# Windowed attention with stacked keys, the band added together with the row maximum, and the division on GpSimd, in a hybrid diffusion transformer step

## The reference, cut to what matters

```python
band = jnp.abs(qi + BLOCK - kj) <= WINDOW
s_loc = jnp.einsum('bqhgd,bmhd->bhgqm', q_blk, k_loc).astype(jnp.float32) * SCALE
s_loc = jnp.where(valid, s_loc, NEG_INF)
s_ctx = jnp.einsum('bqhgd,bchd->bhgqc', q_blk, k_ctx).astype(jnp.float32) * SCALE
p = _sink_softmax(jnp.concatenate([s_loc, s_ctx], axis=-1), sink).astype(v.dtype)
return (jnp.einsum('bhgqm,bmhd->bqhgd', p[..., :3 * BLOCK], v_loc)
        + jnp.einsum('bhgqc,bchd->bqhgd', p[..., 3 * BLOCK:], v_ctx))
```

## Time and profile before

| | us |
|---|---|
| median of 3 runs | 692.92 |
| lowest and highest | 692.34, 694.98 |
| the profiled execution | 693.16 |
| its span in the profile | 691.4 |

### The profile page before, as it was taken

How to read it: one execution, slowest core, us unless ns; L and a number is a source line. 1 busy time by engine, 2 the same in 40 slices (tenths; PEclk the granted TensorE clock), 3 DMA queues, 4 the chain that set the end, 5 groups by cost and what they waited for, 6 DMA issues and landing times.

```text
span 691.4 us, 9619 instructions
## 1 busy us (share of the span) xinstructions
PE 556.6 (81%) x3081; PEld 310.5 (45%) x3082; DVE 204.1 (30%) x540; ACT 155.7 (23%) x375; POOL 123.2 (18%) x183
## 2 busy tenths in 40 slices
PE   0569999999889998999973489899999787878700
PEld 0335654444355664455542245454655444444300
DVE  1240321011567774124447311111111011111027
ACT  2520111011145453233331021111111110111132
POOL 1000000003400000100000423333333232331212
PEclk9999999999989999999995599999999999999955
DMA  8999007081599400400054559999999999999073
GB/s 260 404 389 398 25 5 300 1 306 58 137 357 299 62 0 1 153 0 31 30 220 161 209 216 377 410 365 412 409 416 406 396 408 406 410 416 373 29 306 163
DMA packets 56728, 168.11 MB, mean 243 GB/s; under 512 B 11773, under 2 KB 12389, under 8 KB 55793
## 3 DMA queue, kind: packets, MB, share of 16 engines
q1 hardware_dynamic: 48928, 150.71, 57.4%
q0 software_dynamic: 6752, 14.13, 5.7%
q10 hardware_dynamic: 1008, 2.75, 1.0%
HBM read 161.13 MB, written 14.57 MB: 254 GB/s over the span
## 4 chain that ended last, share of the span: by engine, by line
PE 50%; DMA 27%; DVE 9%; SPq 5%; ACT 3%; issue 3%; PEld 1%; PEldq 0%; POOL 0%; ACTq 0%; POOLq 0%; DVEq 0%
DMA ring<-in_w_down_dram 13%; PE ps L595 10%; PE ps L709 10%; PE ps L817 6%; PE ps L496 5%; PE ps L576 5%; DMA w<-in_w_down_dram 4%; DMA ring<-in_w_up_dram 4%; DMA ring<-in_w_in_dram 3%; PE ps L825 3%; PE ps L660 3%; PE ps L577 2%; PE ps L688 2%; SPq L395 2%; PE ps L515 2%
## 5 line engine op out<-in xcount | busy, mean ns | idle before, releaser
L817 PE MATMUL ps<-ring,xt 128*64 128x256 f32 x768 | 95.0, 404 | 18.6 <-DMA ring<-in_w_up_dram 11.9
L817 PEld LDWEIGHTS ps<-ring,xt 128*64 128x64 f32 x768 | 63.2, 145 | 56.8 <-issue 35.6
L595 PE MATMUL ps<-ring,h_t 128*128 128x512 f32 x160 | 69.5, 593 | 0.0
L1259 DVE TENSOR_TENSOR hid<-act_g,ps 128x128 f32<-128x128 f32 x32 | 9.2, 288 | 188.4 <-ACT act_g L1473 188.4
L709 PE MATMUL ps<-ring,mix_t 128*128 128x512 f32 x120 | 53.2, 594 | 0.0
L595 PEld LDWEIGHTS ps<-ring,h_t 128*128 128x128 f32 x160 | 30.1, 190 | 37.6 <-issue 37.6
L817 PE MATMUL ps<-w,xt 128*64 128x256 f32 x352 | 40.4, 382 | 5.9 <-DMA w<-in_w_up_dram 3.6
L825 PE MATMUL ps<-ring,hid_t 128*64 128x512 f32 x176 | 42.6, 605 | 3.0 <-ACT hid_t L1483 2.5
L576 PE MATMUL ps<-ring,h_t 128*128 128x512 f32 x80 | 41.0, 594 | 3.7 <-DVE h_t L970 2.7
L1567 POOL DMA_INDIRECT xg<-h_rows,idx_in x32 | 33.4, 1044 | 28.2 <-POOL idx_in L1564 26.9
L1577 POOL DMA_INDIRECT expert_results<-y_sb,idx_out x32 | 32.8, 1024 | 28.2 <-POOL idx_out L1574 28.2
(11 more groups left out here) (231 smaller groups left out, 690.3 us busy)
## 6 DMA issues: line engine op xcount, KB each, us to landing
ring<-in_w_mod_dram SPq DMA_DIRECT2D x8, 3072.0 KB, 19.6
ring<-in_w_gate_dram SPq DMA_DIRECT2D x22, 1024.0 KB
ring<-in_w_up_dram SPq DMA_DIRECT2D x22, 1024.0 KB
ring<-in_w_down_dram SPq DMA_DIRECT2D x22, 1024.0 KB
w<-in_w_gate_dram SPq DMA_DIRECT2D x10, 1024.0 KB
w<-in_w_up_dram SPq DMA_DIRECT2D x10, 1024.0 KB
w<-in_w_down_dram SPq DMA_DIRECT2D x5, 1024.0 KB
w_6d<-in_w_down_dram SPq DMA_DIRECT2D x5, 1024.0 KB
```

What stands on the lines that cost most here:

```text
L595: last = pe.matmul(ps[:, 4 + u % 4, :], h_t[:, k, i * P:(i + 1) * P], w[:, k, :], start=(k == 0), stop=(k == KC - 1))
L817: last = pe.matmul(bank[fh * SLOT:(fh + 1) * SLOT, 0:FE].rearrange("p (a f) -> p a f", a=2), x_t[:, k % 4, (k // 4) * SLOT:(k // 4 + 1) * ...
```

## The change

The zero-padded key copies become one tensor `k_t` with both key heads stacked on the partitions. `scores` multiplies 64 partitions of queries by 64 partitions of keys for each key head, the two heads in turn, and no mask product follows. A new fp32 tensor `band` (five blocks: zero, `mask_prev`, zero, `mask_next`, zero) is added by VectorE in the same instruction that takes the maximum: `tensor_tensor_reduce`, once for each key head, writes the masked scores from PSUM to `probs` and the maximum to `att_stats`. It lowers to two instructions, the main one and one that writes the maximum. The exponentials then work in place on `probs`, and `scores(t)` waits for `masked`, not for the exponentials. In tile 1 the key blocks are taken in the order 1, 2, 0, so that a stretch of `band` fits. `normalise` ends with the reciprocal; GpSimd multiplies the two halves of `probs`. `turn_p`, `p_out` and `values` stand one step later. In `scatter` the copy of the row numbers stands ahead of the wait for the expert's result.

```diff
-                return [0] + [1 + m for m in range(max(n - 1, 0), min(n + 2, 4))]
+                return ([5], [1, 2, 0], [0, 1, 2, 3], [0, 2, 3, 4], [0, 3, 4])[i]
...
-                        last = pe.matmul(bank[:, pos * P:(pos + cnt) * P], q, k_t[:, a, first * P:(first + cnt) * P],
-                                         start=(z == 0), stop=(z == len(parts) - 1 and not masks),
-                                         skip_group_check=True)
-                    for z, (pos, m) in enumerate(masks):
-                        last = pe.matmul(bank[:, pos * P:(pos + 1) * P], ident_b[:, :], mask_b[:, m, :],
-                                         start=False, stop=(z == len(masks) - 1), skip_group_check=True)
+                runs = ([(0, 5, 1)], [(0, 1, 2), (2, 0, 1)], [(0, 0, 1), (1, 1, 3)], [(0, 0, 1), (1, 2, 3)],
+                        [(0, 0, 1), (1, 3, 2)])[i]
+                for z, (pos, first, cnt) in enumerate(runs):
+                    for a in range(KVH):
+                        half = slice(a * HD, (a + 1) * HD)
+                        last = pe.matmul(ps[:, 2 * (t % 2) + a, pos * P:(pos + cnt) * P],
+                                         q_t[half, g, i * P:(i + 1) * P], k_t[half, first * P:(first + cnt) * P],
+                                         start=(z == 0), stop=(z == len(runs) - 1), skip_group_check=True)
...
-                        pe.wait_ge(exp_done, t - 1)
+                        pe.wait_ge(masked, t - 1)
...
-                if 2 <= t < NT + 2:
-                    turn_p(t - 2)
...
-                if t >= 4 and t % 2 == 0:
-                    values((t - 4) // 2)
+                if 3 <= t < NT + 3:
+                    turn_p(t - 3)
...
+                if t >= 5 and t % 2 == 1:
+                    values((t - 5) // 2)
...
-            for a in range(KVH):
-                last = dve.tensor_copy(k_t[a * HD:(a + 1) * HD, a, 0:P], ps[a * HD:(a + 1) * HD, 3, 128:256])
-            last.then_inc(s_cols, 1)
+            dve.tensor_copy(k_t[:, 0:P], ps[:, 3, 128:256]).then_inc(s_cols, 1)
...
-                link(dve.tensor_reduce(att_stats[:, MX, t, :], ps[:, 2 * (t % 2):2 * (t % 2) + 2, 0:width(t)], AX_X, ALU.max))
+                if t >= 4:
+                    dve.wait_ge(pt_tr, 2 * (t - 4) + 2)
+                for a in range(KVH):
+                    last = dve.tensor_tensor_reduce(probs[:, t % 4, a, 0:width(t)], ps[:, 2 * (t % 2) + a, 0:width(t)],
+                                                    band[:, m_at:m_at + width(t)], 1.0, -3e38, ALU.add, ALU.max,
+                                                    att_stats[:, MX, t, a:a + 1])
+                last.then_inc(masked, 1)
...
-                link(dve.reciprocal(att_stats[:, INV, t, :], att_stats[:, DEN, t, :]))
-                for a in range(KVH):
-                    p = probs[:, t % 4, a, 0:width(t)]
-                    last = dve.tensor_scalar(p, p, att_stats[:, INV, t, a:a + 1], None, ALU.mult)
-                last.then_inc(p_norm, 1)
+                dve.reciprocal(att_stats[:, INV, t, :], att_stats[:, DEN, t, :]).then_inc(inv_made, 1)
...
+                pool.wait_ge(inv_made, t + 1)
+                for a in range(KVH):
+                    p = probs[:, t % 4, a, 0:w]
+                    last = pool.tensor_scalar(p, p, att_stats[:, INV, t, a:a + 1], 1.0, ALU.mult, ALU.mult)
+                last.then_inc(p_norm, 1)
...
-                pool.wait_ge(y_cp, e + 1)
                 pool.tensor_copy(idx_out[:, c, 0:1], dst_row[:, bass.ds(e, 1)]).then_inc(out_idx, 1)
                 pool.wait_ge(out_idx, e + 1)
+                pool.sem_inc(idx_seen, 1)
+                pool.wait_ge(y_cp, e + 1)
                 pool.sem_inc(idx_seen, 1)
```

More of the change, by code:

```diff
@@ L206, in hybrid_dit_step @@
         d0 = region(9 * KB)
-        k_t = sb("k_t", [P, KVH, 6 * P], F32, d0)
+        k_t = sb("k_t", [P, 6 * P], F32, d0)
+        band = sb("band", [P, 5 * P], F32, d0 + 3 * KB)
         v_all = sb("v_all", [P, 6, KVW], F32, d0 + 6 * KB)
@@ L719, in _ @@
             pe.wait_ge(s_cv, 16)
-            for t in range(NT + 3):
+            for t in range(NT + 4):
                 if t < NT:
                     if t >= 2:
-                        pe.wait_ge(exp_done, t - 1)
+                        pe.wait_ge(masked, t - 1)
                     scores(t)
-                if t == NT + 1:
+                if t == NT + 2:
                     out_proj(0, 0)
-                if 2 <= t < NT + 2:
-                    turn_p(t - 2)
-                if t == NT + 2:
+                if 3 <= t < NT + 3:
+                    turn_p(t - 3)
+                if t == NT + 3:
                     out_proj(0, 1)
-                if t >= 4 and t % 2 == 0:
-                    values((t - 4) // 2)
+                if t >= 5 and t % 2 == 1:
+                    values((t - 5) // 2)
             def turn_use(u):
@@ L1010, in keys_out @@
                 c_at = (5 if i == 0 else i) * P
-                for a in range(KVH):
-                    last = dve.tensor_copy(k_t[a * HD:(a + 1) * HD, a, c_at:c_at + P], ps[a * HD:(a + 1) * HD, 3, 0:P])
-                last.then_inc(qk_dve, 1)
+                dve.tensor_copy(k_t[:, c_at:c_at + P], ps[:, 3, 0:P]).then_inc(qk_dve, 1)
             for i in range(TILES):
@@ L1069, in row_max @@
             def row_max(t):
-                g = t % PAIRS
+                i, g = t // PAIRS, t % PAIRS
+                m_at = 2 * P if i == 1 else 0
                 dve.wait_ge(score_mm, t + 1)
-                link(dve.tensor_reduce(att_stats[:, MX, t, :], ps[:, 2 * (t % 2):2 * (t % 2) + 2, 0:width(t)], AX_X, ALU.max))
+                if t >= 4:
[5 more added lines that the diff above has]
+                last.then_inc(masked, 1)
+                dve.wait_ge(masked, t + 1)
                 ns = nsink[:, :].rearrange("p (a g) -> p g a", a=KVH)[:, g]
@@ L1102, in _ @@
                     normalise(t - 1)
-                if t >= 2:
-                    p_out(t - 2)
-            p_out(NT - 1)
+                if t >= 3:
+                    p_out(t - 3)
+            for t in range(NT - 2, NT):
+                p_out(t)
             def gated(i):
@@ L1385, in exps @@
                 act.activation(att_stats[:, ES, t, :], att_stats[:, SA, t, :], ACT.Exp)
-                if t >= 4:
-                    act.wait_ge(pt_tr, 2 * (t - 4) + 2)
                 for a in range(KVH):
-                    last = act.activation(probs[:, t % 4, a, 0:width(t)], ps[:, 2 * (t % 2) + a, 0:width(t)], ACT.Exp,
+                    last = act.activation(probs[:, t % 4, a, 0:width(t)], probs[:, t % 4, a, 0:width(t)], ACT.Exp,
                                           bias=att_stats[:, NM, t, a:a + 1], scale=SCALE,
@@ L1398, in p_out @@
                 w = width(t)
+                act.wait_ge(pt_tr, 2 * t + 1)
                 act.copy(p_t[:, (t // 2) % 2, 0, 0:w // P, t % 2, :],
@@ L1405, in values_out @@
                 act.copy(mix_t[:, g:g + 2, i * P:(i + 1) * P], ps[:, 4, 0:2 * P].rearrange("p (g q) -> p g q", q=P)).then_inc(pv_cp, 1)
-            for t in range(NT + 3):
+            for t in range(NT + 4):
                 if t < NT:
                     exps(t)
-                if 2 <= t < NT + 2:
-                    p_out(t - 2)
-                if t >= 4 and t % 2 == 0:
-                    values_out((t - 4) // 2)
+                if 3 <= t < NT + 3:
+                    p_out(t - 3)
+                if t >= 5 and t % 2 == 1:
+                    values_out((t - 5) // 2)
             def norms(i):
@@ L1548, in _ @@
                     pool.tensor_tensor(gm_v[:, i - 1], gm_v[:, i - 1], gmn_bc[:], ALU.mult).then_inc(gv_ready, 1)
+            INV = 6
+            for t in range(TILES * PAIRS):
+                i = t // PAIRS
+                w = P * (1 if i == 0 else 3 if i in (1, 4) else 4)
+                pool.wait_ge(inv_made, t + 1)
[3 more added lines that the diff above has]
+                last.then_inc(p_norm, 1)
             pool.wait_ge(pt_tr, 2 * TILES * PAIRS)
```

33 lines of the change are left out of this document (7 added, 26 removed).

## The result

The changed kernel takes 685.68 us (median of 4 runs, 684.39 to 686.62) beside 693.95 for the kernel before on the same chip (4 runs, 692.34 to 696.63). The ratio is 0.9873, 95% interval 0.9850 to 0.9896: faster, by 8.8 us (8.3 by the medians) where 4.9 were forecast. The profiled execution took 684.39, its span 682.5 (before 693.16 and 691.4).

What follows compares the result with a forecast made beforehand. TensorE was taken as nearly full and also waiting on an attention loop through three engines. Attention -4.7 and scatter -0.25 from the profiled 693.16 gave 688.2 us, range 685.0 to 694.0.

Steps and rivals of the forecast that it cites:

- hiding behind the weights: Rival: the experts' weight stream ends at its old time, only the scatter's gain is left; 692.9 us, chance 0.08.
- Scores: Attention's score products: 2.22 to 1.35 us for four blocks, gain 0.87; three blocks to 1.12, gain 0.56.
- No overlap: Rival: TensorE works the two row halves off one by one, 2.00 instead of 1.35; +5.4, 693.6 us, chance 0.12.
- Maximum: VectorE in attention: two instructions with short reads, 1.52 instead of 1.24 us, +0.28, bounds +0.13 and +0.51.
- half-rate rival: New VectorE maximum instruction runs at half rate, 2.5 to 2.6 us with reads; +9.3, 697.5 us, chance 0.10.
- Exponentials: ScalarE in attention: reading SBUF instead of PSUM, 633 against 597 ns, twice, +0.07 us.
- Multiplication on GpSimd: Attention's multiplication by the reciprocal: 0.8 us each, 1.6 a step, bounds 1.1 and 2.6, hidden by the later place.
- wait for GpSimd: Rival: GpSimd's multiplications stretch VectorE's offset operations and sums through the shared port; +2.8, 691.0 us, chance 0.08.
- Depth: Transposes, copies and values one step later in attention: counted as zero, within 0.5 us either way.
- The clock: Fall of TensorE's clock in attention: held unlikely; later warming in tiles 0 and 1 could cost 1 us.
- the slow stretch: First tile and start of tile 1, at granted clock 0.67: -0.9 from scores, -0.9 from VectorE's multiplications.
- Scatter: Row-number copy ahead of the wait, counted at the last expert only: -0.25 us, bounds 0 and -1.1.

Runs made afterwards that it cites:

- depth two: Changed kernel with transposes, copies and values two steps behind the scores instead of three: 689.68 us, ratio 0.9955.
- stacked keys alone: Kernel before with stacked keys only, masks still added by products, transposes two steps behind: 690.24 us, ratio 0.9946.
- the copy first: ScalarE's even copy issued ahead of the exponentials: on the kernel before 691.13 us; on the changed kernel with transposes two steps behind 689.51 us.

## Why the prediction was right, and where it was off

**What bounds the kernel** was read rightly: nearly full **and** waiting on a loop. Both halves were measured later, 8.09 of TensorE's own work in a round of 8.50, and 6.06 in one of 7.53 after the change. That the gain is carried on to the end one to one held: from the first output projection to the last result's copy it takes 386.2 us before (270.12 to 656.29) and 385.1 after (262.51 to 647.65), so hiding behind the weights is refuted.

**Scores**: mechanism right, size off. Forecast 1.35 for four blocks and 1.12 for three; measured 1.09 and 0.88. The halves overlap nearly in full, 1.09 for products that took 2.00 unshared. The narrow piece, which I had priced like four transposes (0.65), is what I overpriced: the wide records start 0.33 after the narrow ones. No overlap is refuted (2.0 expected by it).

**Maximum**: +0.08 measured, +0.28 forecast. The instruction and its read were right (0.686 and 0.083 against 0.684 and 0.08), but two in a row overlap, as the two exponentials with their reads do in the earlier trace rows, which I had noted for ScalarE and not applied here. The half-rate rival is refuted.

**Exponentials**: +0.07, as forecast.

The four-block round therefore lost 0.97 instead of 0.52, the three-block round 0.54 (7.38 in the chain before, 255.90 to 263.28) instead of 0.21. If tile 1's rounds moved like tile 4's, that is 4 x 0.45 + 4 x 0.33 = 3.1 us more than forecast.

**Multiplication on GpSimd**: 0.69 instead of 0.8, two in 1.36, hidden as argued. The forecast said what hides it, "Without the later place the transposes ... would be late": with depth two it is in the chain with 1.37. The offset operations were not stretched, so VectorE doesn't wait for GpSimd here.

**Depth** is the step that failed: "I count zero, within 0.5 us either way." The reasoning was that the round has the same members and that the extra iteration at the end has nothing but transposes. The first holds for the length of the round (8.51 with depth three before the change, 7.57 and 7.53 after it), though with GpSimd's multiplication and two steps its members are others. The second does not: with short scores the end of the attention, from step 16 on, takes 15.8 with three steps and 16.9 to 18.0 with two, about 1.2 of it by the loop and in two kernels about as much by the clock. With what lies before step 8, where depth and clock are not told apart, 3 to 6 us hang on the depth.

**The clock** I held unlikely to fall, since it had stayed at 1.00 with 3.04 of 5 us busy. In the changed kernel it stayed from 210 us on (0.99 and 1.00). In the kernels with depth two it did not always: with stacked keys alone TensorE was busy for 3.04 of the 5 us up to 265 at 0.96 and then had 0.70, with the copy first 2.76 at 1.00 and then 0.66, while the changed kernel with depth two, with 2.75, kept 1.00. The row that I had leaned on doesn't rule a fall out.

**Where the rest of the gain lies.** Counted from the first maximum, the attention is 9.8 us shorter, where the forecast had 4.7: to step 8 4.2 (19.45 to 15.27; forecast about 2.2, the two 0.9 and tile 1's 0.4), from there to step 16 4.2 (32.89 to 28.69; forecast 2.1), and behind it 1.4 (17.15 to 15.76; forecast 0.4). So the middle came out double by the scores and the maximum, and the ends by more than that. In this pair of profiles the later start takes 2.2 of the 9.8 back and the stages behind the output projection add 1.0 and the scatter's 0.25, which gives the 8.9 between the spans. That the time missed the forecast by 3.9 and not by 5 or more is in part the luck of a late start. The terms for the slow stretch, 0.9 from a ratio and 0.9 as half of VectorE's 1.8, stand for 4.2 with the depth in it; no run takes them apart.

**Scatter**: 0.25 in the trace, as forecast (after: copy's end 648.24, transfer 649.09).

**What I missed** is not in the sum: the loop's member that could go for nothing. The even copy stood in the earlier trace rows with 0.49 behind exponentials with which it has no data in common. The same rows that gave the forecast named an edit worth more than the whole change.

## What to carry to other kernels

Write the loop down from the chain of waits and ask of each link whether it is data or only a place in an engine's queue; a link of the second kind goes by an exchange of two lines. Its price depends on the next bound: the same exchange gave 3 us where TensorE's own work stood 0.4 below the round, and 10 where it stood 1.5 below. Parts of a change are not additive: depth alone gave nothing, 3 to 6 us together with short scores; GpSimd's multiplication 2 or less, then 6 to 8. And price several like instructions in a row by what they take together.

## What the runs showed of the hardware

The two halves of the array's rows overlap nearly in full for fp32 products with 64 rows, whatever the order in the program: 1.09 and 1.11 us for what took 2.00 in the kernel before.

A change of the array's shape has a price inside the pieces, where I had seen none. In the kernel before with the copy first, the same four records of scores take 1.07 behind the values and 0.87 behind transposes, and eight transposes 1.09 ahead of the values and 0.88 elsewhere: 0.2 at each side. Behind row-half scores, eight transposes take 1.02, and 0.88 when the masks stand between, whose four products then take 0.34 for 0.22. The Trainium skill (TensorEngine Tiling (Array Packing), "Key Properties") states that changing the mode drains the engine. The prices here, 0.1 to 0.2 a change, agree with it; whether they are a drain or a weight load that is not hidden, no run here tells apart.

An instruction of VectorE that adds a tensor and takes a maximum in one pass, from PSUM, costs what a copy costs: 686 ns for 512 fp32 elements, 554 for 384, and 83 ns for reading the maximum.
